# Moving the weight slots by 32 bytes against the activations, in a one-core residual block in fp32r

## The chip, the cores and the metric

The kernel runs on one core of one Trainium2 chip. The metric is device time in microseconds of one execution. The kernel before was timed twice: 2223.24 and 2224.24 us, median 2223.74 us.

## The reference

One layer on x of 512 tokens by 2048 channels, float32:

```python
h   = RMSNorm(x);  p = h @ w_in            # q, k, v, forget logits, x_rnn, gate_rnn
y_A = forgetting attention, 16 heads of 64
y_B = RG-LRU(causal conv(x_rnn)) * gelu(gate_rnn)
x   = x + RMSNorm(concat(RMSNorm(y_A), RMSNorm(y_B)) @ w_out)
h   = RMSNorm(x)
x   = x + RMSNorm((gelu(causal conv(h @ w_gate)) * (h @ w_up)) @ w_down)
```

The big products are 2048 x 5136 (`w_in`), 2048 x 2048 (`w_out`), twice 2048 x 6144 (`w_gate`, `w_up`) and 6144 x 2048 (`w_down`).

## The kernel before

**Arithmetic.** Every large operand is split in two fp32r parts, a high and a low one, and `product` (lines 1676 to 1678) issues three matmuls into one PSUM bank: high x high, high x low, low x high. The first argument of a matmul is the stationary operand, which a weight load brings in, and the second streams through.

**Weights.** They come in units of 128 x 1024 floats (512 KB), eight tiles of 128 x 128 each. SyncE (in the fast part also GpSimd) loads a unit into `raw` or a buffer like it. ScalarE copies it to the high part of a slot (lines 557, 563, 905), VectorE subtracts that from the raw unit into the low part (lines 996, 1006, 1543), and TensorE works through it, 24 matmuls a unit. Semaphores count the units: `hi_done`, `split_done`, `unit_used`. ScalarE waits with a slot's next unit until TensorE has used the one before in it.

**Slots.** There are two slots in the tensor `w_all`: slot 0 has its high part in the third quarter and its low part in the fourth, slot 1 in the first and the second. The units alternate between them. The down projection has its own views, `wd_hi` and `wd_lo`, of the same tensor. The fast part of the FFN has a third slot, `w_2`, a tensor of its own.

**Stages.** In order of time:

1. The mixer, up to some 530 us: weights stationary (`w_tile`, line 1681), activations `act_hi` and `act_lo` moving, 512 columns. Between the units stand the small products of the heads: the forget gate (lines 1829 and 1830, `f_w` stationary), the gates (`gw_hi`, `gw_lo` stationary, `xc_hi`, `xc_lo` moving), scores (line 1735) and values (lines 1759 and 1760, `v_both` stationary, `pt_hi`, `pt_lo` moving, 512 to 128 columns).
2. The output projection, and from some 740 us the first six hidden tiles of the FFN: as in the mixer.
3. From some 880 us the other 42 hidden tiles: `fast_product` (line 1977) computes them with seven products for eight, of 256 columns. Their weights, partly sums of units, are stationary in the three slots in turn; quadrants of the activations or their sums (`tsum`) move.
4. From some 1650 us the down projection: `down_unit` (line 2016) loads 128 tokens of the hidden activations, kept in `act_hi` and `act_lo`, as the stationary operand, and 512 columns of the weights move. Even units are in slot 0, odd ones in slot 1.
5. The end: scaling, transposes, the residual, the store.

**Addresses.** The tensors lie one behind the other, each rounded up to 32 bytes for a partition. Modulo 512: `w_all` has 16512 bytes, `par` behind it takes 1376, three small ones take 96, and the next ones (`raw`, `ones`, `rms`, `sq`, `acc`, `ident`) are multiples of 512. So `act_hi` begins 64 bytes above the beginning of `w_all`, modulo 512, and `act_lo` and `tsum` have the same place as `act_hi`. A tile of weights is 512 bytes in a partition, a row of activations 2048, and the quadrants and token tiles begin at multiples of 512 from there, so each part keeps its place modulo 512. `xc_hi`, `gw_hi`, `pt_hi`, `v_both` and their neighbours lie 32 above the activations (an `xr` of 2080 bytes stands before them), `w_2` lies 64 above them. `f_w` is a view of `pt_hi[0]` with 256 bytes for each of its 16 tiles.

Of the kernel before, what the change touches and what calls it, by code (L numbers as in the profile page):

```python
# [41 lines left out]
UW = UK * P  # L42
# [53 lines left out]
LINE = 64  # L96
# [36 lines left out]
def block_kernel(nc, xT, par_d, weights, gate_w, out):  # L133
# [3 lines left out]
    with ExitStack() as ctx:  # L137
# [3 lines left out]
        def sb(name, shape, dt=F32):  # L141
            return sb_in(ctx, name, shape, dt)

        def sem(name):
# [3 lines left out]
        w_all = sb("w_all", [4 * UW + 2 * LINE // 4], F32R)  # L148
# [8 lines left out]
        std = sq[:, 1]  # L157
        acc = sb("acc", [S])
        ident = sb("ident", [P])
        w_hi, w_lo = [[w_all[:, UW * c:UW * c + UW] for c in (2 + part, part)] for part in range(2)]  # L160
        wd_hi, wd_lo = [[w_all[:, UW * c + 2 * LINE // 4:UW * c + UW + 2 * LINE // 4] for c in (2 + part, part)]
                        for part in range(2)]
        banks = [ctx.enter_context(nc.psum_tensor(f"bank{i}", [P, S], F32)) for i in range(8)]
        PJ, SB, PT = banks[0:2], banks[2:5], banks[5:8]
        HEAD_BANKS = (SB, PT)
# [1963 lines left out]
```

## Time and profile before

| | us |
|---|---|
| median of 2 runs | 2223.74 |
| profiled execution, its own time | 2222.32 |
| its span | 2220.7 |
| TensorE busy | 2183.4 |
| weight loads | 1928.7 |
| VectorE busy | 1530.0 |
| ScalarE busy | 1002.6 |

The profile's execution is 1.42 us below the median. Engines work side by side, so the busy times don't add up to the span. Matmuls are pipelined: one of 512 columns is shown with some 390 ns, but the next starts some 230 ns after it. The distance of two starts is what a matmul costs in a row of them.

### The profile page before, as it was taken

The page shows a single profiled execution, that of the slowest core. Times are in us where ns is not written, and L with a number is a line of the kernel's source. Part 1 is how long each engine was busy: PE and PEld are TensorE (multiplying, and loading weights), DVE is VectorE, ACT ScalarE, POOL GpSimd, SP SyncE. Part 2 cuts the span into 40 slices and gives each one's busy share as a digit, 9 for nine tenths or more (in the row PEclk, how much of TensorE's full clock was granted, in tenths as well). Part 3 has the DMA queues.
Part 4 walks back from the last instruction along what each step waited for, and adds up shares of the span by engine and source line. Part 5 has one row for each costly group of instructions (what it writes and reads, how often), then busy time and mean ns, then how long its engine had stood idle before and what let it go on. Part 6 is the DMA issues. An engine that isn't in the chain of part 4 may idle for free.

```text
span 2220.7 us, 34413 instructions
## 1 busy us (share of the span) xinstructions
PE 2183.4 (98%) x13320; PEld 1928.7 (87%) x13320; DVE 1530.0 (69%) x2021; ACT 1002.6 (45%) x1274; POOL 140.6 (6%) x207
## 2 busy tenths in 40 slices
PE   7999999999999899999999999999999999999998
PEld 5788888887788688999999999999998888888886
DVE  7677776777855777888888888888885444444445
ACT  5555554457322454444444444444444343343433
POOL 0000000000100000111111111111102000000000
PEclk9999999999999899999999999999999999999999
DMA  5232222222432436777777777777768322323343
GB/s 171 79 93 83 97 87 97 97 91 79 132 124 95 142 109 181 211 208 204 211 207 209 211 212 211 204 202 204 212 179 293 123 95 95 96 98 98 101 165 114
DMA packets 99853, 328.67 MB, mean 148 GB/s; under 512 B 12944, under 2 KB 20240, under 8 KB 99616
## 3 DMA queue, kind: packets, MB, share of 16 engines
q1 hardware_dynamic: 75200, 240.59, 32.1%
q0 software_dynamic: 22240, 82.36, 17.0%
q10 hardware_dynamic: 2304, 4.20, 0.5%
q8 instruction: 77, 1.26, 0.2%
q14 instruction: 32, 0.26, 0.0%
HBM read 306.09 MB, written 21.00 MB: 147 GB/s over the span
## 4 chain that ended last, share of the span: by engine, by line
PE 91%; DVE 5%; issue 2%; ACT 1%; DMA 1%; POOL 0%; SPq 0%; DVEq 0%; ACTq 0%; POOLq 0%
PE bank L1676 29%; PE bank L1677 29%; PE bank L1678 29%; DVE w_all L996 1%; PE bank L1735 1%; PE bank L1748 1%; DMA raw<-weights 1%; ACT w_all L557 1%; DVE x_b L1667 0%; DVE act_lo L1332 0%; PE bank L1760 0%; PE bank L1759 0%; DVE act_lo L1011 0%; DVE xc L1185 0%; PE bank L1706 0%
## 5 line engine op out<-in xcount | busy, mean ns | idle before, releaser
L1676 PE MATMUL bank<-act_hi,w_all 128*128 128x512 f32 (+1 forms) x1760 | 620.0, 352 | 19.7 <-DVE act_lo L1011 14.2
L1678 PE MATMUL bank<-act_hi,w_all 128*128 128x512 f32 (+1 forms) x1760 | 614.3, 349 | 0.0
L1677 PE MATMUL bank<-act_lo,w_all 128*128 128x512 f32 (+1 forms) x1760 | 612.4, 348 | 0.0
L1676 PEld LDWEIGHTS bank<-act_hi,w_all 128*128 128x128 f32 x1760 | 332.1, 189 | 67.9 <-issue 20.1
L1678 PEld LDWEIGHTS bank<-act_hi,w_all 128*128 128x128 f32 x1760 | 331.8, 189 | 46.7
L1677 PEld LDWEIGHTS bank<-act_lo,w_all 128*128 128x128 f32 x1760 | 332.0, 189 | 44.1 <-issue 0.2
L1006 DVE TENSOR_TENSOR w_all<-raw,w_all 128x1024 fp32r<-128x1024 f32 x96 | 117.7, 1226 | 286.8 <-ACT w_all L563 286.8
L1677 PE MATMUL bank<-w_all,act_hi 128*128 128x512 f32 x768 | 302.3, 394 | 0.0
L1676 PE MATMUL bank<-w_all,act_hi 128*128 128x512 f32 x768 | 301.0, 392 | 1.2 <-DVE w_all L1006 1.2
L1678 PE MATMUL bank<-w_all,act_lo 128*128 128x512 f32 x768 | 298.7, 389 | 0.0
L996 DVE TENSOR_TENSOR w_all<-raw,w_all 128x1024 fp32r<-128x1024 f32 x136 | 166.5, 1224 | 156.6 <-ACT w_all L557 154.8
L1676 PE MATMUL bank<-tsum,w_all 128*128 128x256 f32 x896 | 247.4, 276 | 0.0
L1677 PE MATMUL bank<-tsum,w_all 128*128 128x256 f32 x896 | 247.3, 276 | 0.0
L1678 PE MATMUL bank<-tsum,w_all 128*128 128x256 f32 x896 | 247.3, 276 | 0.0
L563 ACT ACTIVATE w_all<-raw 128x1024 fp32r<-128x1024 f32 x96 | 101.8, 1060 | 295.8 <-PE bank L1678 283.3
L557 ACT ACTIVATE w_all<-raw 128x1024 fp32r<-128x1024 f32 x136 | 143.6, 1056 | 185.0 <-PE bank L1678 182.6
L905 ACT ACTIVATE w_all<-raw_s 128x1024 fp32r<-128x1024 f32 x112 | 119.1, 1063 | 154.2 <-PE bank L1678 151.1
L1676 PEld LDWEIGHTS bank<-w_all,act_hi 128*128 128x128 f32 x768 | 144.2, 188 | 35.5 <-DVE w_all L1006 1.4
L1678 PEld LDWEIGHTS bank<-w_all,act_lo 128*128 128x128 f32 x768 | 144.2, 188 | 31.8
L1677 PEld LDWEIGHTS bank<-w_all,act_hi 128*128 128x128 f32 x768 | 144.4, 188 | 29.3
L1543 DVE TENSOR_TENSOR w_all<-raw_s,w_all 128x1024 fp32r<-128x1024 f32 x112 | 137.3, 1226 | 46.6 <-ACT w_all L905 45.4
L1676 PEld LDWEIGHTS bank<-tsum,w_all 128*128 128x128 f32 x896 | 168.2, 188 | 0.0
(264 smaller groups left out, 3659.5 us busy)
## 6 DMA issues: line engine op xcount, KB each, us to landing
raw<-weights SPq DMA_DIRECT2D x310, 512.0 KB, 3.5
raw_s<-weights SPq DMA_DIRECT2D x84, 512.0 KB, 4.7
raw_s<-weights POOLq DMA_DIRECT2D x84, 512.0 KB, 6.0
raw_a<-weights SPq DMA_DIRECT2D x42, 512.0 KB, 5.0
h_spill<-h_out POOLq DMA_DIRECT2D x48, 256.0 KB, 3.6
h_t<-h_spill POOLq DMA_DIRECT2D x24, 512.0 KB, 7.2
x<-xT POOLq DMA_DIRECT2D x16, 256.0 KB, 3.1
out<-x ACTq DMA_DIRECT2D x16, 256.0 KB, 2.2
```

The source lines that it names most:

```text
L557: act.activation(w_hi[s], raw[:, s], ACT.Copy).then_inc(hi_done, 1)
L563: act.activation(wd_hi[s], raw[:, s], ACT.Copy).then_inc(hi_done, 1)
L905: act.activation(w_slot(q)[0], RAW_OF[n](i), ACT.Copy).then_inc(hi_done, 1)
L996: dve.tensor_tensor(w_lo[s], raw[:, s], word(w_hi[s]), ALU.subtract).then_inc(split_done, 1)
L1006: dve.tensor_tensor(wd_lo[s], raw[:, s], word(wd_hi[s]), ALU.subtract).then_inc(split_done, 1)
L1543: dve.tensor_tensor(lo, RAW_OF[n](i), word(hi), ALU.subtract).then_inc(split_done, 1)
L1676: pe.matmul(dst, ah, bh, start=start, stop=False, skip_group_check=goes_on)
L1677: pe.matmul(dst, ah, bl, start=False, stop=False, skip_group_check=goes_on)
L1678: return pe.matmul(dst, al, bh, start=False, stop=stop, skip_group_check=goes_on)
L1735: last[e] = pe.matmul(dst, q, k, start=t == 0, stop=t == 2)
L1748: last = pe.transpose(dst, sm[:, c:c + P], ident[:])
```

## The change

Both slots begin at another place within `w_all`, whose size (4128 elements) stays. Before, the slots began at the quarters, and in the down projection 128 bytes behind them. Now slot 0 is shifted by 96 bytes and slot 1 by 32, in the down projection slot 0 by 128 as before and slot 1 by 96. Against the activations modulo 512, slot 0 goes from 64 below to 32 above, slot 1 from 64 below to 32 below; in the down projection slot 0 stays 64 above and slot 1 goes from 64 above to 32 above.

```diff
--- before.py
+++ after.py
@@ -157,9 +157,13 @@
         std = sq[:, 1]
         acc = sb("acc", [S])
         ident = sb("ident", [P])
-        w_hi, w_lo = [[w_all[:, UW * c:UW * c + UW] for c in (2 + part, part)] for part in range(2)]
-        wd_hi, wd_lo = [[w_all[:, UW * c + 2 * LINE // 4:UW * c + UW + 2 * LINE // 4] for c in (2 + part, part)]
-                        for part in range(2)]
+        def slots(shift_0, shift_1):
+
+            at = [[UW * (2 + part) + shift_0 // 4, UW * part + shift_1 // 4] for part in range(2)]
+            return [[w_all[:, a:a + UW] for a in ats] for ats in at]
+
+        w_hi, w_lo = slots(LINE + LINE // 2, LINE // 2)
+        wd_hi, wd_lo = slots(2 * LINE, LINE + LINE // 2)
         banks = [ctx.enter_context(nc.psum_tensor(f"bank{i}", [P, S], F32)) for i in range(8)]
         PJ, SB, PT = banks[0:2], banks[2:5], banks[5:8]
         HEAD_BANKS = (SB, PT)
```

## Rows read from the trace of the kernel before

**Rows 1.** The page: busy time by engine, granted clock in 40 slices, the last chain.

```profile
PE 2183.4 (98%) x13320; PEld 1928.7 (87%) x13320; DVE 1530.0 (69%) x2021; ACT 1002.6 (45%) x1274; POOL 140.6 (6%) x207
...
PEclk9999999999999899999999999999999999999999
...
PE 91%; DVE 5%; issue 2%; ACT 1%; DMA 1%; POOL 0%; SPq 0%; DVEq 0%; ACTq 0%; POOLq 0%
PE bank L1676 29%; PE bank L1677 29%; PE bank L1678 29%; DVE w_all L996 1%; PE bank L1735 1%; PE bank L1748 1%; DMA raw<-weights 1%; ACT w_all L557 1%; DVE x_b L1667 0%; DVE act_lo L1332 0%; PE bank L1760 0%; PE bank L1759 0%; DVE act_lo L1011 0%; DVE xc L1185 0%; PE bank L1706 0%
```

**Rows 2.** Waits of TensorE: us in total, times, longest.

```profile
PE bank L1676 <- DVE w_all L996: 3.2, 3, 1.7
```

**Rows 3.** Stretches: length, TensorE busy (matmuls), granted clock, DMA share, GB/s.

```profile
600.00:700.00 100.00, 100.00 (x438) 1.00 0.36 118
...
1050.00:1640.00 590.00, 590.00 (x5209) 1.00 0.77 208
1700.00:2190.00 490.00, 490.00 (x2142) 1.00 0.33 111
```

**Rows 4.** Order of time in the fast part: start, length, instruction.

```profile
1200.03 0.28 PE L1676 MATMUL bank<-tsum,w 128*128 128x256 f32 x1
1200.04 0.19 PEld L1677 LDWEIGHTS bank<-tsum,w 128*128 128x128 f32 x1
```

**Rows 5.** TensorE in order of time where w_2 hands over to w_all.

```profile
882.81 0.28 PE L1676 MATMUL bank<-tsum,w 128*128 128x256 f32 x1
...
884.51 0.28 PE L1676 MATMUL bank<-act_hi,w_all 128*128 128x256 f32 x1
...
887.01 0.28 PE L1677 MATMUL bank<-act_lo,w_all 128*128 128x256 f32 x1
```

**Rows 6.** TensorE by line and shape: count, busy us, mean ns, idle before.

```profile
L1676 PE MATMUL bank<-act_hi,w_all 128*128 128x512 f32 x1088 | 434.6, 399 | 19.7 <-DVE act_lo L1011 14.2 <-DVE w_all L996 3.2 <-DVE act_lo L1332 2.3
...
L1676 PE MATMUL bank<-w_all,act_hi 128*128 128x512 f32 x768 | 301.0, 392 | 1.2 <-DVE w_all L1006 1.2
...
L1676 PE MATMUL bank<-tsum,w_all 128*128 128x256 f32 x896 | 247.4, 276 | 0.0
...
L1676 PE MATMUL bank<-act_hi,w_all 128*128 128x256 f32 x672 | 185.5, 276 | 0.0
```

**Rows 7.** VectorE by line and shape.

```profile
L996 DVE TENSOR_TENSOR w_all<-raw,w_all 128x1024 fp32r<-128x1024 f32 x136 | 166.5, 1224 | 156.6 <-ACT w_all L557 154.8
...
L1380 DVE TENSOR_TENSOR o<-o 128x512 f32<-128x512 f32 x16 | 11.1, 692 | 0.5
...
L1192 DVE TENSOR_TENSOR xc_lo<-xc,xc_hi 128x512 fp32r<-128x512 f32 x8 | 5.5, 692 | 2.5 <-ACT xc_hi L624 2.5
```

**Rows 8.** Order of time, the forget-gate projection: its second matmul, what follows the last.

```profile
42.01 0.39 PE L1830 MATMUL bank<-act_lo,pt_hi 128*64 128x512 f32 x1
...
45.48 0.59 PE L1706 MATMUL bank<-acc,ones 128*128 128x512 f32 x1
```

**Rows 9.** Order of time, the gates of one pair: the first, what follows the sixth.

```profile
184.58 0.40 PE L1676 MATMUL bank<-xc_hi,gw_hi 128*128 128x512 f32 x1
...
185.97 0.39 PE L1676 MATMUL bank<-act_hi,w_all 128*128 128x512 f32 x1
```

**Rows 10.** Order of time, the values of two heads, their 256-column matmuls.

```profile
180.08 0.29 PE L1759 MATMUL bank<-pt_hi,v_both 128*128 128x256 f32 x1
180.21 0.28 PE L1760 MATMUL bank<-pt_lo,v_both 128*128 128x256 f32 x1
180.32 0.23 PE L1759 MATMUL bank<-pt_hi,v_both 128*128 128x128 f32 x1
...
181.37 0.28 PE L1759 MATMUL bank<-pt_hi,v_both 128*128 128x256 f32 x1
181.49 0.28 PE L1760 MATMUL bank<-pt_lo,v_both 128*128 128x256 f32 x1
181.60 0.22 PE L1759 MATMUL bank<-pt_hi,v_both 128*128 128x128 f32 x1
```

**Rows 11.** Order of time, sums over channels in fp32.

```profile
577.91 1.02 PE L1706 MATMUL bank<-acc,ones 128*128 128x512 f32 x2
578.77 1.02 PE L1706 MATMUL bank<-acc_b,ones 128*128 128x512 f32 x2
```

## The prediction

> **What bounds the kernel now.** I read the page's busy table and its chain first. TensorE is busy 98% of a span of 2220.7 us at a granted clock of 0.9 or more in all slices but one, and the chain that ended last runs through it for 91%, 29% on each of the three lines of `product` [rows 1]. The waits of TensorE for a weight slot are 3.2 us in three places [rows 2]. So almost nothing is waited for: the time is the number of matmuls times the distance between two starts, and that distance is what a changed address could touch.
>
> The distances come from three stretches without a pause [rows 3]. A row counts every matmul that overlaps the stretch, so I add one matmul's length (0.39 or 0.28 us) to it. Output projection: 100.39 / 438 = 229.2 ns. Fast part of the FFN, 256 columns: 590.28 / 5209 = 113.3 ns. Down projection: 490.39 / 2142 = 228.9 ns. I use 229.0 ns for 512 columns and 113.3 ns for 256. Twice 113.3 is 226.6, so 512 columns cost 2.4 ns more in one piece than in two.
>
> A weight load starts 0.01 us after a matmul starts, and it loads the next one's stationary operand [rows 4]. Two streams therefore read SBUF together, and only their relative place can matter. Counted from the activations modulo 512, and by the order of allocation, that place is today: loads 64 bytes below the moving operand in the mixer, the output projection and the FFN's opening; 64 below for `w_all` and 64 above for `w_2` in the fast part; and in the down projection, where the weights move and the activations are loaded, again loads 64 below. In the fast part the 15 matmuls up to 884.51 us go by `w_2` (`w` in the rows; 1.70 us, 113.3 ns each) and the 22 behind them by `w_all` (2.50 us, 113.6 ns) [rows 5]. So 64 above and 64 below cost the same within the rows' rounding.
>
> **The change part by part.** Nothing is added or removed on any queue. The splits, their waits, the DMAs into `raw` and the order of the matmuls are the same, and only destinations and sources move.
>
> The affected matmuls [rows 6]: 3 x 1088 = 3264 of 512 columns load from `w_all`, half from each slot. 3 x (896 + 672) = 4704 of 256 columns load from it. 3 x 768 = 2304 move weights in the down projection, and only slot 1 is shifted there, 1152 of them. `w_2` stays.
>
> ScalarE and VectorE now write slots that begin 32 bytes off a multiple of 64. VectorE's splits into `xc_lo`, which already lies so, take 692 ns, and a sum of the same shape on aligned tiles takes 692 too [rows 7]. I take zero for both engines. The cover is that TensorE waits 3.2 us for weights in all; were it gone, 1% on a split of 1.22 us [rows 7] would be 12 ns for each 24 matmuls, 0.5 ns a matmul.
>
> What the trace has at other distances:
> - The forget-gate projection loads `f_w`, at 32 bytes above the activations (and 288, in turns). 15 starts in 45.48 - 42.01 = 3.47 us are 231.3 ns, 2.3 more than 229.0 [rows 8]. It loads 64 columns, not 128. This is the nearest row to slot 0.
> - The gates have both operands at the same place modulo 512: 1.39 us for 6, 231.7 ns, 2.7 more [rows 9].
> - The head values, the same place too, at 256 columns: 0.24 us and 0.23 us for two, 117.5 ns, 4.2 more than 113.3 [rows 10].
>
> Prices. Slot 0 at +32: bounds are -2.4 ns (512 columns as cheap as two halves) and +2.7 (gates). I take +2.3, from the row that has just that distance: 1632 x 2.3 = 3.8 us. Slot 1 at -32 has no row. It lies between -64 (no price) and 0 (+2.7), so I take half, 1.35, with the same bounds: 1632 x 1.35 = 2.2 us. Down slot 1: the loads are now 32 below the moving weights, the same distance, so 1.35 again: 1152 x 1.35 = 1.6 us. Fast part, 4704: the bounds are 0 and +4.2. I take 0, because +64 and -64 both give 113.3 and because in the priced row both operands lie off the line, not the load alone. The sum is +7.6 us. The gates' row is weighed once more here: 229.0 against 231.7 says that place counts for something.
>
> By the Trainium skill (SBUF — State Buffer, "Who interferes with whom") TensorE has two independent read ports, one for the moving operand and one for the weights, and never waits on anyone; by that rule the sum would be zero. The gates' row speaks against it by 2.7 ns, the two sides of 64 bytes for it.
>
> The sum is made against the profiled execution: 2222.32 + 7.6 = 2229.9. The median of the runs is 2223.74, 1.4 above that execution, so the forecast is **2231 us**.
>
> **The rivals.**
> - Place does not matter at this size. For it: +64 and -64 agree. Against it: the gates. 2224 us.
> - The 2.4 ns that 512 columns have over two halves are a collision, and 32 bytes end it. For it: 256 columns show no such extra beside the same loads. Against it: the three other distances show more, not less. 4416 x 2.4 = 10.6 us, 2213 us.
> - Any slot off the 64-byte step costs what the gates and the values cost, in every stage: 2.7 x 4416 + 4.2 x 4704 = 11.9 + 19.8 = 31.7 us, 2255 us. For it: every row with an operand so placed is slower. Against it: in the values both operands are so placed, and each row follows a change of shape.
> - **The slower side.** A 256-column matmul spends 113.3 / 16 = 7.1 ns on 64 bytes of its moving operand. If an operand that starts in the middle of such a piece costs one piece more, at each load and at each moving operand, it is 7.1 x (4416 + 4704) = 64.8 us, 2288 us. Its place is the fast part and the mixer alike. It decides over the 2% from 44.5 / 9120 = 4.9 ns a matmul. Against it: no row above shows over 4.2.
> - **The faster side.** The whole excess over plain streaming is a collision. Sums by fp32 matmuls of 512 columns come two in 0.86 us [rows 11], 430 each; if those are two passes of 215, the stream needs 215 for 512 and 107.5 for 256. 14.0 x 4416 + 5.8 x 4704 = 61.8 + 27.3 = 89 us, 2135 us. Against it: 113.3 at -64 and +64, and nothing near 215 at 0 or +32. The Trainium skill (TensorE: Matmul & The Clock Gate, "Back-to-back issue gap") gives N / 2.4 + 2.5 ns, 215.8 for 512 and 109.2 for 256. By that the gain would be an estimated 77 us.
> - That the change does not do what it says is all but excluded: the slots are plain slices, and the buffer has 4128 elements, which the shifted ones (up to 2048 + 32 + 2048) just fill.
>
> **How the numbers follow.** The small loss has 0.40, no effect 0.22, the small gain 0.25, the full loss 0.07, the slower side 0.03, the faster side 0.03. The likeliest's own range is 2224 to 2240. For 8 in 10 I need the small gain (2213, and some 4 us for a slightly larger one) and the full loss (2255): 2209 to 2256. About what this measurement can tell from no change is 2%, 44 us. Only the two last rivals pass it, so faster 0.03, slower 0.03, within 0.94.
>
> **What would show it.** In the changed kernel the same three stretches give the steps. The output projection should have a distance of 230 to 231 ns, the down projection 229.5, the fast part 113.3. A fast part at 115 or more means the full loss, at 120 the slower side. A distance of 226.6 in the 512-column stages means the small gain. If 113.3 falls, the faster side is true. The down projection should alternate, units of slot 1 slower than units of slot 0; if the two are equal, my price by place is wrong. VectorE's 1224 ns for a split should stay. The forecast is wrong if the fast part moves at all, since its 4704 matmuls weigh most and I priced them at nothing.

## The result and the profile after

The changed kernel takes 2255.65 us (2 runs, 2254.97 to 2256.33), against 2223.74 before: ratio 1.0145, 95% interval 1.0123 to 1.0166. It is 32 us slower. Its lines 1680 to 1682 are the three matmuls of `product` (1676 to 1678 before), line 1000 is the split by VectorE (996 before).

The page of the changed kernel, against [rows 1]:

```profile
span 2253.3 us, 34413 instructions
PE 2217.0 (98%) x13320; PEld 1944.6 (86%) x13320; DVE 1530.3 (68%) x2021; ACT 1002.8 (45%) x1274; POOL 140.3 (6%) x207
...
PEclk9999999999999999999999999999999999999999
...
PE 91%; DVE 5%; issue 2%; ACT 1%; DMA 1%; POOL 0%; SPq 0%; DVEq 0%; ACTq 0%; POOLq 0%
```

There are as many instructions as before, the busy time of VectorE and ScalarE and the chain's shares are the same, and the clock is no lower. TensorE alone is busy 34 us longer. Its waits, against [rows 2], and a split by VectorE, against [rows 7], have not moved:

```profile
PE bank L1680 <- DVE w_all L1000: 3.0, 3, 1.5
```
```profile
L1000 DVE TENSOR_TENSOR w_all<-raw,w_all 128x1024 fp32r<-128x1024 f32 x136 | 166.6, 1225 | 162.7 <-ACT w_all L561 161.0
```

So it is the distance between starts. Stretches without a pause in the changed kernel (length, TensorE busy and matmuls, granted clock, DMA share, GB/s), against [rows 3]:

```profile
600.00:700.00 100.00, 100.00 (x430) 1.00 0.35 115
1050.00:1640.00 590.00, 590.00 (x5083) 1.00 0.75 203
1730.00:2190.00 460.00, 460.00 (x1993) 1.00 0.32 112
```

Worked out as in the prediction: 100.39 / 430 = 233.5 ns in the output projection (229.2 before), 590.28 / 5083 = 116.1 ns in the fast part (113.3), 460.39 / 1993 = 231.0 ns in the down projection (228.9). In the fast part one can read each slot's own distance from the first matmuls of successive units of 24, `w_2` (`w`), slot 0, slot 1, `w_2` again:

```profile
965.44 0.28 PE L1680 MATMUL bank<-tsum,w 128*128 128x256 f32 x1
...
968.16 0.28 PE L1680 MATMUL bank<-tsum,w_all 128*128 128x256 f32 x1
...
971.00 0.28 PE L1680 MATMUL bank<-act_hi,w_all 128*128 128x256 f32 x1
...
973.80 0.28 PE L1680 MATMUL bank<-act_hi,w 128*128 128x256 f32 x1
```

`w_2`, which did not move, takes 2.72 us a unit as before; slot 0 takes 2.84 and slot 1 2.80. Averaged over all units of the stage, the distances are 113.4, 118.4 and 116.6 ns. The down projection alternates too (the first matmuls of a unit in slot 0, one in slot 1, and the next):

```profile
1902.32 0.39 PE L1680 MATMUL bank<-w_all,act_hi 128*128 128x512 f32 x1
...
1907.81 0.40 PE L1680 MATMUL bank<-w_all,act_hi 128*128 128x512 f32 x1
...
1913.40 0.39 PE L1680 MATMUL bank<-w_all,act_hi 128*128 128x512 f32 x1
```

Slot 0, unmoved, takes 5.49 us and slot 1 5.59 us: 228.9 and 233.0 ns.

By stage, from the first to the last matmul of each in the two traces: the start of the fast part went from 873.3 to 881.7 us (+8.4), the fast part from 799.9 to 819.3 (+19.4), the down projection from 527.7 to 532.5 (+4.8). That is 32.6, the whole difference of the two spans. (The down projection begins at 1674.6 us in the trace before, later than the 1650 of the list of stages.)

### The profile page after: what moved, and what is told of

Same layout as the page of the kernel before. It is cut to its first block, busy times and chain, and to the rows that moved or that the text cites. A ratio compares the mean times of both kernels' runs of the same rounds, so it can differ in the third digit from the quotient of the medians.

```text
span 2253.3 us, 34413 instructions
## 1 busy us (share of the span) xinstructions
PE 2217.0 (98%) x13320; PEld 1944.6 (86%) x13320; DVE 1530.3 (68%) x2021; ACT 1002.8 (45%) x1274; POOL 140.3 (6%) x207
## 4 chain that ended last, share of the span: by engine, by line
PE 91%; DVE 5%; issue 2%; ACT 1%; DMA 1%; POOL 0%; SPq 0%; DVEq 0%; ACTq 0%; POOLq 0%
PE bank L1680 29%; PE bank L1682 29%; PE bank L1681 29%; DVE w_all L1000 1%; PE bank L1739 1%; PE bank L1752 1%; DMA raw<-weights 1%; ACT w_all L561 1%; DVE x_b L1671 0%; DVE act_lo L1336 0%; PE bank L1764 0%; PE bank L1763 0%; DVE act_lo L1015 0%; DVE xc L1189 0%; PE bank L1710 0%
## 5 line engine op out<-in xcount | busy, mean ns | idle before, releaser
L1681 PE MATMUL bank<-act_lo,w_all 128*128 128x512 f32 (+1 forms) x1760 | 619.3, 352 | 0.0
L1010 DVE TENSOR_TENSOR w_all<-raw,w_all 128x1024 fp32r<-128x1024 f32 x96 | 117.6, 1225 | 291.7 <-ACT w_all L567 291.6
L1000 DVE TENSOR_TENSOR w_all<-raw,w_all 128x1024 fp32r<-128x1024 f32 x136 | 166.6, 1225 | 162.7 <-ACT w_all L561 161.0
L1680 PE MATMUL bank<-tsum,w_all 128*128 128x256 f32 x896 | 250.9, 280 | 0.0
L1681 PE MATMUL bank<-tsum,w_all 128*128 128x256 f32 x896 | 250.9, 280 | 0.0
L1682 PE MATMUL bank<-tsum,w_all 128*128 128x256 f32 x896 | 250.7, 280 | 0.0
L909 ACT ACTIVATE w_all<-raw_s 128x1024 fp32r<-128x1024 f32 x112 | 119.0, 1063 | 165.0 <-PE bank L1682 162.2
```

Source lines behind the costliest of these rows:

```text
L909: act.activation(w_slot(q)[0], RAW_OF[n](i), ACT.Copy).then_inc(hi_done, 1)
L1000: dve.tensor_tensor(w_lo[s], raw[:, s], word(w_hi[s]), ALU.subtract).then_inc(split_done, 1)
L1010: dve.tensor_tensor(wd_lo[s], raw[:, s], word(wd_hi[s]), ALU.subtract).then_inc(split_done, 1)
L1680: pe.matmul(dst, ah, bh, start=start, stop=False, skip_group_check=goes_on)
L1681: pe.matmul(dst, ah, bl, start=False, stop=False, skip_group_check=goes_on)
L1682: return pe.matmul(dst, al, bh, start=False, stop=stop, skip_group_check=goes_on)
```

## The experiments

"Place" is where the load lies from the moving operand, modulo 512 bytes. Distances per slot are means of start to start between the 24 matmuls of a unit, without steps of 300 ns and more; for the output projection they are taken in its stretch without pauses. Which steps are taken in moves them by up to 0.3 ns. Kernels with an interval were run 4 to 10 times, the others (e7, e8, e9, e11, e12) once. The distances of every kernel come from one execution.

**Each part of the change alone.**

```diff
-        w_hi, w_lo = slots(LINE + LINE // 2, LINE // 2)
-        wd_hi, wd_lo = slots(2 * LINE, LINE + LINE // 2)
+        w_hi, w_lo = slots(96, 32)      # e1; e2: slots(0, 0)
+        wd_hi, wd_lo = slots(128, 128)  # e1; e2: slots(128, 96)
```

> The slots of the mixer, the output projection and the FFN shifted as in the changed kernel (96 and 32 bytes), the down projection as before (128 and 128). In the changed kernel's trace the distance of two starts is 233.2 ns for 512 columns (229.0 before), 118.4 and 116.6 ns for 256 columns in slots 0 and 1 (113.4 before), and 233.0 ns in slot 1 of the down projection (228.9). Theory P (the relative place of load and moving operand, modulo 512) and theory L (an operand that begins off a multiple of 64 bytes in SBUF costs more, wherever the other lies) agree here: 4.2 x 3264 + 5.0 x 2352 + 3.2 x 2352 = 33 us at most, less what old waits cover: +27 to +33 us, down projection at 228.9. A rival that the stages act on one another (through slots that overlap otherwise) would give another sum than the two parts.

> Only slot 1 of the down projection shifted (96 instead of 128 bytes), the rest as before. P and L: slot 1 of the down projection at 233.0 ns, slot 0 at 228.9, all else as before: 4.1 x 1152 = 4.7 us, 2228. If the parts act on one another: anything else.

e1 took 2252.81 us, ratio 1.0135 (1.0118 to 1.0152), with 118.4, 116.6, 233.3 ns and 228.9 in the down projection. e2 took 2227.5 us, ratio 1.0022 (1.0013 to 1.0032). The two parts add: 29.9 + 4.6 = 34.5 beside 31.9 for both at once, within the intervals. In e2 the slot that was moved pays, and only while it is read (first matmuls of a unit in slot 1, in slot 0, and the next):

```profile
1902.26 0.40 PE L1680 MATMUL bank<-w_all,act_hi 128*128 128x512 f32 x1
...
1907.86 0.39 PE L1680 MATMUL bank<-w_all,act_hi 128*128 128x512 f32 x1
...
1913.35 0.40 PE L1680 MATMUL bank<-w_all,act_hi 128*128 128x512 f32 x1
```

5.60 us, then 5.49. ScalarE and VectorE fill slot 1 while TensorE works in slot 0, so their writes to the shifted addresses cost TensorE nothing. It is the reading.

**The fast part alone**, by views of its own for `w_slot` (e10).

```diff
+        w_hi, w_lo = slots(0, 0)
+        wd_hi, wd_lo = slots(128, 128)
+        f_hi, f_lo = slots(96, 32)
...
-            return (w_2[:, 0], w_2[:, 1]) if k == 2 else (w_hi[k], w_lo[k])
+            return (w_2[:, 0], w_2[:, 1]) if k == 2 else (f_hi[k], f_lo[k])
```

> Only the fast part has the changed slots (96 and 32), by views of its own; the 512-column stages are as before. The changed kernel's fast part is 19.4 us longer than that of before (first to last matmul of 256 columns: 819.3 against 799.9 us). If that is its own: 2223 + 19.4 = 2242, ratio 1.0087, slots at 118.4, 116.6 and 113.4. If part of it was carried over from the shifted stages before it: less.

2242.64 us, ratio 1.0090 (1.0073 to 1.0107), the fast part 819.3 us. As expected for a cost of its own: 61% of the loss lies here.

**Relative place, or the step of 64 bytes?** In the changed kernel the shifted slots are both near the other operand and off a multiple of 64 bytes. e3 separates the two by placing everything alike, e4 by shifting both operands.

```diff
+        w_hi, w_lo = slots(64, 64)      # e3
+        wd_hi, wd_lo = slots(64, 64)    # e3
```
```diff
-        w_all = sb("w_all", [4 * UW + 2 * LINE // 4], F32R)
+        w_all = sb("w_all", [4 * UW + 2 * LINE // 4 + 8], F32R)   # e4
+        w_hi, w_lo = slots(32, 32)      # e4
+        wd_hi, wd_lo = slots(160, 160)  # e4
```

> All slots of w_all at the same place modulo 512 as the activations (shift 64 everywhere), all on multiples of 64 bytes; w_2 stays 64 above. Theory L: no operand is off the 64-byte step, so 229.0 and 113.4 ns stay, 2224 us. Theory P: the two streams are as close as can be, so it costs at least what 32 bytes cost: 512 columns at 233 or more in every slot, the down projection's slot 0 too, 256 columns at 118 or more, w_2 at 113.4: 4.2 x 5568 + 5.0 x 4704 = 47 us, 2270 us or more. By the gates' row of before (same place, but off the 64-byte step) only 2.7 ns and 4.2 ns: 2259.

> w_all is 32 bytes longer, so that everything behind it lies 32 bytes further, and all slots are shifted by 32 more: every relative place is as before (64 below, 64 above), but both operands of every large matmul begin 32 bytes off a multiple of 64; the gates and the values, which were off it, are on it now. Theory P: 2224 us, distances 229.0 and 113.4 ns, gates as before at 231.7. Theory L: every matmul pays, w_2's too: 4.2 x 5568 + 4.1 x 7056 = 52 us, 2276 us, and the gates fall to 229.0.

e3 took 2254.88 us, ratio 1.0144 (1.0127 to 1.0161), but not in the way that either theory said. Its stretches:

```profile
600.00:700.00 100.00, 100.00 (x443) 1.00 0.36 116
1050.00:1640.00 590.00, 590.00 (x4949) 1.00 0.74 196
1730.00:2190.00 460.00, 459.68 (x2029) 1.00 0.35 117
```

100.39 / 443 = 226.6 ns and 460.07 / 2029 = 226.7 ns: the 512-column stages are faster than before. The fast part is at 590.28 / 4949 = 119.3 ns, 120.0 in both slots and 117.8 in `w_2`, though `w_2` has not moved. Theory L is out, and P as I had it (near is dear) holds for 256 columns only.

e4 took 2222.93 us, ratio 0.9994 (0.9982 to 1.0006). The gates, now on the step, took 232.1 ns, on average as before.

```profile
600.00:700.00 100.00, 100.00 (x430) 1.00 0.37 115
1050.00:1640.00 590.00, 590.00 (x5209) 1.00 0.77 208
1730.00:2190.00 460.00, 459.90 (x2010) 1.00 0.33 107
```

Fast part and down projection are where they were, so being off the step costs nothing there. One stage disagrees: the output projection is at 100.39 / 430 = 233.5 ns, with every place unchanged. In this execution the fast part starts at 875.4 us, 2.1 us later than in the trace before. The ten timed runs don't show that: their median is 0.02 us from that of the kernel before, the interval ends at +1.3 us, and the profiled run is the slowest of the ten (2224.01 us).

**The output projection's other distance.** e11 shifts everything by 64 bytes instead of 32.

```diff
+        w_all = sb("w_all", [4 * UW + 2 * LINE // 4 + 16], F32R)
+        w_hi, w_lo = slots(64, 64)
+        wd_hi, wd_lo = slots(192, 192)
```

> Everything behind w_all and all slots 64 bytes further: places, and the 64-byte step, as before. With 32 bytes further the output projection alone went to 233.3 ns at an unchanged relative place, while the mixer stayed at 229.0. If being off the 64-byte step did that: 229.0 here in every 512-column stage, 2223 us. If the same place allows two steady patterns and the start picks one: the output projection may stand at 233 here too.

2222.49 us, and all stages as before, the output projection at 228.9:

```profile
600.00:700.00 100.00, 100.00 (x439) 1.00 0.37 118
```

So relative place is not the whole story: with the same place the output projection stood at 229.0 in four kernels (before, e2, e10, e11) and at 233.3 in one. The 32 bytes are not needed for that. In e4 itself the first unit of the output projection takes 5.50 us (540.52 to 546.02, 229 ns); 233.3 comes only behind the pauses that follow. And the mixer of e2 has every address of the kernel before. Here is its second unit in the two traces (its first matmul and the next unit's), the kernel before first:

```profile
17.98 0.40 PE L1676 MATMUL bank<-act_hi,w_all 128*128 128x512 f32 x1
...
23.58 0.40 PE L1676 MATMUL bank<-act_hi,w_all 128*128 128x512 f32 x1
```
```profile
18.22 0.39 PE L1680 MATMUL bank<-act_hi,w_all 128*128 128x512 f32 x1
...
23.72 0.39 PE L1680 MATMUL bank<-act_hi,w_all 128*128 128x512 f32 x1
```

5.60 against 5.50 us, 233 against 229 ns, at the same addresses. Of the 94 units without a pause (no step of 250 ns or more) that the mixer, the output projection and the FFN's opening have, 7 stand at 233 in the trace before and 87 at 229; in e2 none stands at 233, in e4 26 do, and in the changed kernel and in e1 all 94. With 512 columns, then, the place before allows two levels, and at the changed places only the upper one was seen. What picks the level was not tested.

**The two best places together** (e5).

```diff
+        w_hi, w_lo = slots(64, 64)
+        wd_hi, wd_lo = slots(64, 64)
+        f_hi, f_lo = slots(128, 0)
...
-            return (w_2[:, 0], w_2[:, 1]) if k == 2 else (w_hi[k], w_lo[k])
+            return (w_2[:, 0], w_2[:, 1]) if k == 2 else (f_hi[k], f_lo[k])
```

> The mixer, the output projection, the FFN's opening and the down projection with both slots at the same place as the activations (shift 64); the fast part by views of its own, slot 0 at 64 above (128), slot 1 at 64 below (0). With everything at the same place the trace gave 226.8 ns for 512 columns (229.0 before) and 120.0 for 256 (113.4 before, w_2 117.8). Theory P, each stage for itself: 226.8 and 113.4 ns in all three slots of the fast part: 2.2 x 5568 = 12 us below before, 2211. Rival: a steady pattern is carried over from one stage to the next (w_2, unmoved, was slower there): the fast part stays above 113.4, and at 117.8 for its 7056 matmuls it would be 31 us more, 2242.

2213.4 us, ratio 0.9957 (0.9943 to 0.9970) to the kernel before. **This beats both kernels.**

```profile
600.00:700.00 100.00, 100.00 (x443) 1.00 0.36 116
1050.00:1640.00 590.00, 590.00 (x5209) 1.00 0.77 208
1730.00:2190.00 460.00, 459.55 (x2028) 1.00 0.32 104
```

226.6, 113.3 and 459.94 / 2028 = 226.8 ns. `w_2` is back at 113.4: its 117.8 in e3 hung on the slots that take turns with it, not on the stages before. The gain is 9.4 us of the 12 expected. Up to the fast part it is 5.2 us and in the down projection 4.2; the mixer's slot 0 stands at 229.4 on average, since it has most of the breaks, and steps of 230 to 283 ns stand behind them, in the trace before too.

e12 shifts this arrangement by 32 bytes as e4 did.

```diff
+        w_all = sb("w_all", [4 * UW + 2 * LINE // 4 + 8], F32R)
+        w_hi, w_lo = slots(96, 96)
+        wd_hi, wd_lo = slots(96, 96)
+        f_hi, f_lo = slots(160, 32)
```

> The fastest arrangement so far (512-column stages at the same place, fast part 64 above and 64 below), with everything behind w_all and every slot 32 bytes further: no place changes, but every large operand begins 32 bytes off a multiple of 64. If only places count: 226.8 and 113.4 ns as without the 32 bytes, some 2213 us. If the step counts in the output projection, which went from 229.0 to 233.3 with 32 bytes more while its place stayed: it stands above 226.8 here, by up to 4 ns for its 640 matmuls and more, 2 to 3 us.

2213.35 us in the one run, at 226.8 and 113.4 ns in all the large stages but the mixer's slot 0 (229.5 as in e5), the output projection among them. At this place the step makes no difference.

**Both sides of 64** (e6).

```diff
+        w_hi, w_lo = slots(128, 0)
+        wd_hi, wd_lo = slots(128, 0)
```

> Slot 0 at 64 above, slot 1 at 64 below, in all stages; all on multiples of 64. If 64 bytes to either side are alike for 512 columns too: 229.0 and 113.4 ns in both slots everywhere, 2224 us. If the side counts (the order in which the two streams reach a piece): slot 0 of the mixer, or slot 1 of the down projection, whose loads are then 64 above the moving weights, differs from 229.0.

2233.54 us, ratio 1.0048 (1.0033 to 1.0063). The fast part is at 113.3 in all slots. With 512 columns the side counts. Output projection, slot 1 (64 below) and then slot 0 (64 above), by the first matmul of each unit:

```profile
602.75 0.39 PE L1680 MATMUL bank<-act_hi,w_all 128*128 128x512 f32 x1
...
608.25 0.39 PE L1680 MATMUL bank<-act_hi,w_all 128*128 128x512 f32 x1
...
613.84 0.39 PE L1680 MATMUL bank<-act_hi,w_all 128*128 128x512 f32 x1
```

5.50 against 5.59 us, inside the units 228.9 against 233.2 ns. Slot 1 keeps its 229 in 48 of its 62 units without a pause; 14 stand at 233, 6 of them among the 11 of the FFN's opening. In the down projection slot 1, whose loads are then above the moving weights, is at 233.0.

**By part** (e7).

```diff
+        w_hi = [w_all[:, 2 * UW + 8:3 * UW + 8], w_all[:, 0:UW]]
+        w_lo = [w_all[:, 3 * UW + 32:4 * UW + 32], w_all[:, UW + 8:2 * UW + 8]]
+        wd_hi, wd_lo = slots(128, 128)
```

> High and low parts of a slot at different places, down projection as before. Slot 0: high 32 below, low 64 above. Slot 1: high 64 below, low 32 below. Two loads of three are of the high part. If each load pays for its own place: in the fast part slot 1 at 113.4 + 3.2 / 3 = 114.5 ns and slot 0 at 113.4 + 3.2 x 2 / 3 = 115.5; with 512 columns 230.4 and 231.8, and the surplus stands in the step whose load is off. If one load off its place puts the whole row of matmuls into the slower pattern: 116.6 and 233.2 in both slots.

2252.11 us. The fast part stands at 119.0 (slot 0) and 117.5 (slot 1), `w_2` at 114.0; with 512 columns both slots are at 231.3. Neither expectation holds. With 256 columns one shifted load in three costs more than three did at that place (117.5 against 116.6); with 512 columns one or two in three cost about half. A price for each load on its own does not describe it; the matmuls of a row act on one another in a way that this run does not explain.

**Other distances** (e8: 16, 48 and 96 bytes; e9: 96 and 128).

```diff
+        w_hi, w_lo = slots(80, 48)       # e8
+        wd_hi, wd_lo = slots(112, 80)    # e8
-        sb_in(ffn, "line_of_2", [LINE // 4])
+        sb_in(ffn, "line_of_2", [LINE // 4 + 8])      # e8; e9: [2 * LINE // 4]
+        w_all = sb("w_all", [4 * UW + 2 * LINE // 4 + 16], F32R)   # e9
+        w_hi, w_lo = slots(32, 0)        # e9
+        wd_hi, wd_lo = slots(32, 0)      # e9
```

> Distances of 16 and 48 bytes and of 96: slot 0 16 above, slot 1 16 below; in the down projection the loads 48 below (slot 0) and 16 below (slot 1) the moving weights; w_2 96 above. If the price falls evenly from the same place to 64 bytes: 256 columns at 16 bytes between 120.0 and 118.4 (slot 0) and 120.0 and 116.6 (slot 1); 512 columns between 226.8 and 233.2, some 230; down 48 below some 231; w_2 at 113.4. If 64-byte pieces decide and the order within them doesn't: 16, 32 and 48 alike, 118.4, 116.6, 233.2; w_2 at 96 is then off a piece too, at 116 to 118.

> Distances of 96 and 128 bytes. Everything behind w_all lies 64 bytes further, w_2 another 64. Loads of slot 0 are 96 below, of slot 1 128 below; in the down projection loads are 96 above (slot 0) and 128 above (slot 1) the moving weights; w_2 is 128 above. So far, at 256 columns: 113.4 at 64 to either side, 120.0 at 0, 118.1 and 117.3 at 16, 118.4 and 116.6 at 32, 118.7 at 96 above. Theory S (a whole number of 64-byte pieces other than none is cheap, anything between is not): slot 1 and w_2 at 113.4, slot 0 at 116 to 119; at 512 columns 233 in slot 0 and some 229 in slot 1. Theory D (nearness decides, and w_2's 118.7 came from its neighbours in the turn, whose slots were at 16): all three slots at 113.4 and 229 everywhere.

e8 took 2261.52 us, e9 2282.44 us, the slowest of all. Neither expectation of e8 holds: the two sides of 16 bytes differ by 5 ns with 512 columns (233.4 and 228.3), neither of them near 230, 48 and 16 below differ in the down projection (230.1 and 231.8), and `w_2` at 96 above is at 118.7. In e9 theory S and theory D both fail: with loads 128 bytes away, all three slots of the fast part are slow (first matmuls of `w_2`, slot 0, slot 1, `w_2`):

```profile
969.39 0.28 PE L1680 MATMUL bank<-tsum,w 128*128 128x256 f32 x1
...
972.24 0.28 PE L1680 MATMUL bank<-tsum,w_all 128*128 128x256 f32 x1
...
975.12 0.27 PE L1680 MATMUL bank<-act_hi,w_all 128*128 128x256 f32 x1
...
977.96 0.28 PE L1680 MATMUL bank<-act_hi,w 128*128 128x256 f32 x1
```

2.85, 2.88 and 2.84 us a unit, where 2.72 is what 64 bytes give. All distances found (ns; down projection: load against moving weights):

| place of the load | 256 columns | 512, output projection | 512, down projection |
|---|---|---|---|
| 128 below | 118.5 | 233.1 | |
| 96 below | 119.7 | 233.3 | |
| 64 below | 113.4 | 229.0 (e4: 233.3) | 228.9 |
| 48 below | | | 230.1 |
| 32 below | 116.6 | 233.3 | 233.0 |
| 16 below | 117.3 | 228.3 | 231.8 |
| same | 120.0 | 226.8 | 226.7 |
| 16 above | 118.1 | 233.4 | |
| 32 above | 118.4 | 233.1 | |
| 64 above | 113.4 | 233.2 | 233.0 |
| 96 above | 118.7 | | 234.0 |
| 128 above | 118.7 | | 232.4 |

The table gives what was found in a slot, not what its place alone costs. The slots that take turns are not always at the same place in one kernel, and e3's `w_2` shows that a neighbour can matter by 4.4 ns. In the fast part 96 and 128 were seen only beside neighbours at 16, 96 or 128, so that 128 bytes by themselves are dear is not shown. The 512-column values are levels of one stage: 16 above (e8) stands at 233 in 25 of its 32 units without a pause and at 227 in the other 7.

## Why the prediction came out as it did

The forecast was 2231 with a range of 2209 to 2256. The measured 2255.65 lies at its very edge. The direction was right, the chance of a change within 2% too, and the time that came is that of a rival to which I gave 0.07, the full loss: 2255. That it lies inside the range at all is luck: the upper end was that rival's time, and its reason, that a slot off the 64-byte step pays, is refuted by e4 (off the step, no slower) and e3 (on it, 32 us slower). Its prices from the gates and the values were near only in sum: 11.9 and 19.8 us against the measured 8.4 + 4.8 = 13.2 and 19.4. By the sign that the prediction itself gave, a fast part that moves at all, the forecast was wrong.

- **What bounds it** held. Distance between starts made all of the difference. No wait, no split and no transfer moved.
- **The fast part, 4704 matmuls at nothing**, is the step that failed. It measured +5.0 ns in slot 0 and +3.2 in slot 1, 2352 x 5.0 + 2352 x 3.2 = 19.3 us, and the stage grew by 19.4. I took the 64 above and 64 below of [rows 3, 5] as the two ends of a flat range. They are two good places with bad ones between and outside (table). The values' +4.2 of [rows 10] was within 1 ns of both, but it was read at another place (0, where long rows cost +6.6 in e3) and from short groups, so that is luck too.
- **512 columns, stationary weights** were under-priced. I had 2.3 and 1.35 ns, and it was +4.2 in the output projection in both slots (233.1 to 233.3 against 229.0). Up to the fast part +8.4 us came instead of 6.0; 4.2 x 3264 would be 13.7. The mixer's steps without a break grew by 3.3, 5.2 and 3.2 ns (first to second matmul, second to third, third to the next), 3.9 on average; the rest is in the steps with breaks, and their length differs from one execution to the next. e1, with the same addresses up to there, starts its fast part at 884.1 us, 10.8 later than the kernel before. So the 8.4 of one trace is good to some 2 us.
- **Down projection, slot 1**: 1.35 priced, 4.1 measured, 4.7 us for 1152 matmuls (4.8 from the trace, 4.6 by e2's time). "Half of the zero distance, because it lies between" was the error again: the price does not fall evenly with distance. With 512 columns the same place is even the best one.
- **That the gates' 231.7 (both at the same place) is a price of the place** was wrong. In e3 long rows of matmuls at that place run at 226.8. The gates are six matmuls between others, and 231.7 is the price of a change from one row to another at least in part; they took 232.1 in e4 and 229.7 in e3, where only the slots of the products around them had moved.
- **The small gain** as a rival (2.4 ns over two halves is a collision) named a real thing and the wrong place: it ends at distance zero (226.8 against twice 113.3), not at 32. e5 shows 9.4 us of the 10.6 that I had put on fewer matmuls.
- **ScalarE and VectorE at nothing** held: 1225 ns a split against 1224, 2.72 us a unit in `w_2`. (TensorE's waits for weights were not 3.2 us in all: [rows 6] have 1.2 more for the splits of the down projection.)
- **A whole further piece at each matmul, 7.1 ns**, was not seen at 32 bytes. The largest surplus over the kernel before in any arrangement is 120.0 - 113.4 = 6.6 ns, and that stands on multiples of 64 bytes.
- **The faster side** did not come: no stretch of any run is below 226.6 ns with 512 columns or 113.3 with 256. (The second estimate there adds up to 78 us, not 77.)
- The rule of the Trainium skill (SBUF — State Buffer, "Who interferes with whom") that TensorE, with independent read ports for the moving operand and the weights, never waits on anyone, would have given no change. The traces do not agree with a change of nothing: with the same instructions and only other addresses the distance goes from 113.4 to 120.0 and from 226.8 to 234.0 ns. What does agree is that the writes of ScalarE and VectorE to the moved slot cost it nothing more (e2: 228.9 ns in slot 0 while slot 1 is filled).

Shown: the cost lies in the reading by TensorE, depends mostly on relative place, and is another for 256 and 512 columns. In the changed kernel it follows the slot that is read, and it repeats: 118.4 and 116.6 ns in its fast part, in e1 and in e10, 233.0 in the down projection's slot 1 there and in e2. Open: the mechanism. That the load and the moving stream collide in SBUF is an inference from place alone, and no run without one of the streams was made. Open too are what picks one of two levels at one place, how a neighbour acts, and whether the places repeat after 512 bytes: all tiles lie a multiple of 512 apart, so no run could tell.

## What to carry to other kernels

When TensorE is busy without a pause, its time is count times distance, and in this kernel the addresses of stationary and moving operand relative to each other are worth up to 6% of a 256-column distance and 3% of a 512-column one. Do not interpolate between places: measure each shape at a few (here the same place modulo 512 for 512 columns, 64 bytes to either side for 256), and give each stage its own view of the buffer. Take a price from a row in the middle of a long uniform run, not from six matmuls between others, and read it in several stages and executions, since one place can show two levels.

## What was not expected of the hardware

At the same place modulo 512, 512-column matmuls are fastest (226.8 ns) and 256-column ones slowest (120.0). For 512 columns the two sides of 64 bytes differ (229.0 below, 233.2 above). Farther apart was not better: with all slots 96 or 128 bytes off the fast part stood at 118.5 to 119.7, where 64 bytes give 113.4. An unmoved slot was slowed by those that take turns with it (`w_2`, 117.8 in e3, 113.4 in e5). And at one and the same place units of 512-column matmuls stood at 229 or at 233 ns, in one execution (87 and 7 of 94 units before) and differently in two executions with the same addresses.
